# Final scaling of token blocks 0 and 2 moved from VectorE to ScalarE and GpSimd

## What is computed

```
def hier_moe(...):
    ...
    y_rows = lax.map(expert_block, (x_rows, block_e)).reshape(n_rows, D)
    y = jax.ops.segment_sum(y_rows * row_w[:, None], row_tok, num_segments=T)

x = x + hier_moe(...)                    # each token adds its two experts' rows, weighted
out = x * rsqrt(mean(x * x) + EPS) * g   # the last RMS norm, g = norm_final_g_2, width 1024
```

## Time and profile before

| | us |
|---|---|
| median of 3 runs | 2687.91 |
| the three runs | 2687.55, 2687.91, 2689.4 |
| the profiled execution, its own time | 2690.0 |
| its span, first to last instruction | 2688.4 |

### The profile page before, as it was taken

The page is one execution under the profiler, slowest core; times in us unless marked ns, Lnnn a source line. Parts: engine busy times, 40 slices in busy tenths (PEclk is TensorE's granted clock), DMA queues, the critical chain, the costliest instruction groups (busy, mean ns, idle before and its releaser), DMA issues. The chain is left out here.

```text
span 2688.4 us, 37345 instructions
## 1 busy us (share of the span) xinstructions
PE 2543.7 (95%) x13135; PEld 1258.4 (47%) x13359; DVE 1925.0 (72%) x3258; ACT 1215.4 (45%) x1283; POOL 1107.7 (41%) x806
## 2 busy tenths in 40 slices
PE   7989999999999999999999899999999699999994
PEld 4565444444444444444444444555544344444441
DVE  5465797776776626888888754466543599999996
ACT  5444232333323323333333343444432488888884
POOL 2000028877878856888888200000000433344331
PEclk9999999999999999999999999999999799999997
DMA  9701334344444467999999532222114499999995
GB/s 387 301 32 75 122 134 157 134 169 154 143 156 149 143 236 265 372 374 371 368 372 379 199 126 95 93 65 77 63 50 154 157 410 391 396 396 403 408 405 220
DMA packets 141756, 611.73 MB, mean 228 GB/s; under 512 B 30657, under 2 KB 47297, under 8 KB 91969
## 3 DMA queue, kind: packets, MB, share of 16 engines
q1 hardware_dynamic: 57312, 411.62, 40.1%
q0 software_dynamic: 48480, 114.61, 11.9%
q10 hardware_dynamic: 35840, 83.90, 8.3%
HBM read 542.73 MB, written 71.50 MB: 228 GB/s over the span
## 5 line engine op out<-in xcount | busy, mean ns | idle before, releaser
L744 PE MATMUL ps<-a_hi,w_lo 128*128 128x512 bf16 (+3 forms) x1740 | 639.4, 370 | 1.8 <-issue 0.2
L743 PE MATMUL ps<-a_lo,w_hi 128*128 128x512 bf16 (+3 forms) x1736 | 637.8, 370 | 3.3 <-issue 0.8
L742 PE MATMUL ps<-a_hi,w_hi 128*128 128x512 bf16 (+3 forms) x1715 | 629.7, 370 | 8.4 <-ACT xn L1531 2.7
L626 POOL DMA_INDIRECT gate_dram<-arena x384 | 469.7, 1223 | 251.1 <-DVE arena L2119 121.8
L742 PE MATMUL ps<-w_hi,arena 128*128 128x512 bf16 (+1 forms) x1326 | 506.7, 382 | 26.1 <-DVE arena L2463 15.2
L743 PE MATMUL ps<-w_lo,arena 128*128 128x512 bf16 (+1 forms) x1327 | 505.2, 381 | 0.9
L744 PE MATMUL ps<-w_hi,arena 128*128 128x512 bf16 (+1 forms) x1327 | 505.1, 381 | 0.9
L2053 DVE TENSOR_TENSOR w_lo<-w_st,w_hi 128x2048 bf16<-128x2048 f32 x127 | 290.7, 2291 | 225.6 <-ACT w_hi L1525 225.6
L1525 ACT ACTIVATE w_hi<-w_st 128x2048 bf16<-128x2048 f32 x127 | 242.6, 1910 | 351.2 <-PE ps L744 314.2
L1531 ACT ACTIVATE xn<-ps 128x512 f32<-128x512 f32 x128 | 76.4, 597 | 425.9 <-PE ps L744 407.8
L742 PEld LDWEIGHTS ps<-a_hi,w_hi 128*128 128x128 bf16 x1768 | 173.9, 98 | 196.6 <-issue 8.0
(11 more groups left out here) (398 smaller groups left out, 3699.3 us busy)
## 6 DMA issues: line engine op xcount, KB each, us to landing
w_st<-in_w_all SPq DMA_DIRECT2D x260, 1024.0 KB
arena<-in_w_all SPq DMA_DIRECT2D x64, 1024.0 KB
act_dram<-xn ACTq DMA_DIRECT2D x64, 512.0 KB, 2.7
xn<-in_w_all SPq DMA_DIRECT2D x32, 1024.0 KB, 9.0
gate_dram<-xn POOLq DMA_DIRECT2D x16, 1536.0 KB, 43.1
arena<-act_dram ACTq DMA_DIRECT2D x64, 384.0 KB, 6.4
arena<-gate_dram ACTq DMA_DIRECT2D x64, 384.0 KB, 7.7
a_hi<-in_w_all SPq DMA_DIRECT2D x16, 1024.0 KB, 7.9
```

Of the source, the lines that this page charges most:

```text
L626: pool.indirect_dma_start(gate_cells, bass.IndirectOffsetOnAxis(ap=place[:, b - 1, j:j + 1], axis=0), shared[:, b - 1, j:j + 1], None).the ...
L742: pe.matmul(dst, l_hi, r_hi, start=start, stop=False)
L743: pe.matmul(dst, l_hi, r_lo, start=False, stop=False)
L744: return pe.matmul(dst, l_lo, r_hi, start=False, stop=stop)
```

## The change

The final scaling of blocks 1 and 3 stays on VectorE. That of blocks 0 and 2 is split: VectorE takes the reciprocal only, ScalarE multiplies the block by it into `xn`, and GpSimd multiplies `xn` by `row` in place. SyncE's stores keep their order and wait for whichever engine finishes the block. The semaphores `rt_x`, `pk_hi` and `pk_lo` are used again, counting on from their earlier values.

```diff
--- before.py
+++ after.py
@@ -564,7 +564,10 @@
             more_passes(sp, one_pass)
 
             for tb in range(TB):
-                sp.wait_ge(end_done, tb + 1)
+                if tb % 2:
+                    sp.wait_ge(end_done, tb // 2 + 1)
+                else:
+                    sp.wait_ge(pk_lo, TB + tb // 2 + 1)
                 sp.dma_start(out[tb * P:(tb + 1) * P, :], xn[:, tb, :]).then_inc(cols_ld, 16)
             sp.wait_ge(cols_ld, 16 * (1 + TB))
 
@@ -731,6 +734,11 @@
                                                 bass.IndirectOffsetOnAxis(ap=to_y[:, s, tb:tb + 1], axis=0)).then_inc(yg_ld[tb], 16)
 
             more_passes(pool, one_pass, gather_outputs)
+
+            pool.wait_ge(row_ld[1], 16 * 3)
+            for tb in range(0, TB, 2):
+                pool.wait_ge(pk_hi, TB + tb // 2 + 1)
+                pool.tensor_tensor(xn[:, tb, :], xn[:, tb, :], row[:, 1, :], ALU.mult).then_inc(pk_lo, 1)
 
 
         @block.tensor
@@ -1781,6 +1789,9 @@
 
             for tb in range(TB):
                 norm(5, tb, res_done, 2 * TB + tb + 1)
+                if tb % 2:
+                    act.wait_ge(rt_x, 1 + tb // 2 + 1)
+                    act.activation(xn[:, tb - 1, :], res[:, tb - 1, :], ACT.Copy, scale=rstd[:, tb - 1:tb]).then_inc(pk_hi, 1)
 
 
         @block.vector
@@ -2512,8 +2523,12 @@
                     if s == 0:
                         dve.drain()
                 last.then_inc(res_done, 1)
-                if tb:
-                    normalise(5, tb - 1, done=end_done)
+                if tb == 2:
+                    dve.wait_ge(row_ld[1], 16 * 3)
+                    normalise(5, 1, done=end_done)
+                elif tb:
+                    dve.wait_ge(sd_done, TB * 5 + tb)
+                    dve.reciprocal(rstd[:, tb - 1:tb], sd[:, tb - 1:tb]).then_inc(rt_x, 1)
             normalise(5, TB - 1, done=end_done)
```

## The result

Over 20 executions of each kernel the median went from 2687.05 to 2692.71 us. The ratio is 1.0022, with a 95% interval of 1.0013 to 1.0031, that is 3.5 to 8.3 us more. The changed kernel is slower by a little. The forecast was 2691.9, 4.0 us more. The first three executions of before, which the prediction had, gave 2687.91; the 20 spread from 2683.78 to 2695.36, so scatter is wider than those three showed.

What follows compares the result with a forecast made beforehand. VectorE was taken as the bound from block 1's adds to E, then ScalarE, VectorE and the store. 2682.85 + 9.56 = 2692.4 against 2688.4 gave 4.0 us more, put on the median 2687.91: 2691.9, range 2688.8 to 2693.6.

Steps and rivals of the forecast that it cites:

- Block 2's adds start 1.20 earlier, with the gather as the next limit: VectorE, tail: without block 0's scaling, block 2's adds start 1.20 us earlier, at 2674.43, their gather landing at 2674.40.
- E: End of VectorE's last add of block 3 in the tail, 2682.27 in the kernel before, forecast 2682.85 after the change.
- Block 2's scaling gains nothing: VectorE behind E: removing this scaling is worth nothing, since it filled a wait for ScalarE's root, ending E + 1.54.
- ScalarE's copy: Copy with a scale: 1.18 us, hidden for block 0; for block 2 from E + 1.44 to E + 2.62, unhidden.
- GpSimd's product: 2.13: GpSimd's product of a block with the weight row, taken as 2.13 us from the 128x1024 subtraction.
- Contention: GpSimd's product of block 0 holds VectorE's scaling of block 1 until 1.08 us after it; 1.20 gained becomes 0.58 lost.
- The end, E + 9.56: Behind E: block 2's product ends at E + 5.21, two stores' data take 2.6 us, span ends E + 9.56.
- Rival B: Block 0's product doesn't hold VectorE: GpSimd starves until E or the two don't meet; +2.2 us; chance 0.34.
- Rival C: GpSimd's product is longer and counts twice: slower by over 0.2% (5.4 us) from a length of 2.83 us; chance 0.10.
- Rival D: Not slower: block 2's store is out before block 3's scaling ends, so 1.20 us is saved, 2686.7; chance 0.03.
- If anything ahead of 2670 moves: Sign named in advance that the prediction is wrong: anything in the profile ahead of 2670 us, before the tail, moves.
- Within 0.2%, at 0.86: Whole-kernel time: chance 0.86 that the change stays within 0.2% (5.4 us), counted as no change.

## Why the prediction was right

The direction and the place were right, and so was the size within the measurement: 4.0 us forecast, 4.3 in the tail of the profile and 5.7 (3.5 to 8.3) in the medians. That the absolute time is closer, 2692.71 for 2691.9, is luck: the three runs of before that it was added to lay 0.86 above the median of 20. By its steps:

- *Block 2's adds start 1.20 earlier, with the gather as the next limit.* Right: 1.07 earlier. In the kernel with the first product held until E they waited 0.53 us for their gather, and E came 0.75 earlier from S than before, not 1.20. Even free of contention this part of the change can't pay what it removes.
- *Block 2's scaling gains nothing.* Right: block 2 alone leaves S to E at 10.63, as before.
- *ScalarE's copy: 1.18, hidden for block 0, at E + 1.44 for block 2.* 1.13, and E + 1.45. No table load came with either copy.
- *GpSimd's product: 2.13.* Too short. 2.35 beside an idle VectorE, 2.20 from the end of the instruction that held it. This and block 2's later start are the 0.2 by which S to E is above the 11.2 summed (2682.85 less 2671.64).
- *Contention: the scaling ends 1.08 after the product.* Exact: 2682.28 less 2681.20. It is the step that turned the gain ahead of E into a loss, and both sides of it were shown: by the order in time and by the operand's memory.
- *The end, E + 9.56.* E + 9.66. The stores behind one another were measured at 1.38 us, for the 1.3 taken.
- *Rival B, that GpSimd starves,* got 0.34. The two kernels that moved the product's start showed no starving. The doubt itself had ground: 17 of the 31 additions at line 683 missed a turn. By the Trainium skill (SBUF — State Buffer, Who interferes with whom) the engine that starts first shuts the other out for that one instruction. The tail's rows agree, and those 17 do not. Had B been true, the end would have been 2.2 later and not 4.3.
- *Rival C, a much longer product,* is out: 2.35 against the 2.83 that it needed.
- *Rival D, not slower,* is out: block 2's product ended at E + 5.29, where it needed E + 3.08.
- *"If anything ahead of 2670 moves"* the prediction was to be wrong. S lies 1.79 later in the changed profile, so by its letter this sign came. It was a poor sign to name: the kernels below, alike up to S, differ by as much.
- *Within 0.2%, at 0.86.* The measured ratio of 1.0022 lies on the other side of that line, though its interval reaches across, and the tail's 4.3 us are 0.16%. I had judged scatter by three runs that lay 1.85 us apart; 20 runs of one kernel span over 11. The chance of a reading beyond the line should have been larger.

What stays open: 1.4 us between the tail's 4.3 and the medians' 5.7. The interval covers it, and no run located it. Ahead of S the profiled kernels of one job, whose instructions are the same up to there, differ by more: block 1's adds began at 2666.71, 2668.42 and 2668.82 in the kernels with only block 0 moved, only block 2 moved and the first product held until E.

## What to carry to other kernels

Look for what stands behind the work that you move: an instruction on the bound engine is worth removing only if what comes next is ready, and one that already fills a wait is worth nothing. GpSimd is no free place for work beside a VectorE that reads two SBUF tiles. VectorE did the whole scaling of a block in 1.28 us, and stood still for 1.86 us when GpSimd did the product for it. With one operand in PSUM the scaling was not held, and the loss fell to the 0.93 us of the adds behind it. At the end of a kernel, count stages and stores per block: here a block among the last that passed three engines cost 3.5 us.

## What the runs showed that I had not expected

In the tail GpSimd got its turn even between two VectorE instructions that follow without a gap, its product ending 2.21 us after the first of them, though in the loop its small addition missed its turn in 17 cases out of 28. And an instruction of VectorE dispatched 20 ns after GpSimd's waits for the whole of it (3.41 us), whereas the same scaling with its weight row in PSUM shows no delay at all (1.28 us).
